# Encoder trunk with four token mixers on one core: where the transposes and value products stand in the opening of the MLA attention

## What is computed

```
hn = rms_norm(h, attn_norm_g[l])
proj = hn @ w_in[l]                      # 4 mixers read column groups of proj
y_a = mla_mixer(...)                     # 8 heads, latent attention
y_b = ssd_mixer(...)                     # Mamba-2, both directions
y_c = diff_mixer(...)                    # differential attention, 4 heads
y_d = mlstm_mixer(...)                   # chunkwise mLSTM, both directions, 4 heads
h = h + concatenate([y_a, y_b, y_c, y_d]) @ w_out[l]
hn = rms_norm(h, ffn_norm_g[l]);  gate, up = split(hn @ w_ffn_in[l])
h = h + (silu(gate) * up) @ w_ffn_out[l]
```

```
q = apply_partial_rope(rms_norm(q, q_head_g), cos, sin)
k = apply_partial_rope(rms_norm(k, k_head_g), cos, sin)
h = rms_norm(h, out_g).reshape(b, t, MLSTM_HEADS * MLSTM_V)
return jax.nn.sigmoid(o_raw) * h
```

## Time and profile before

| | before |
|---|---|
| median of 3 runs | 2541.05 us (2537.44 to 2541.64) |
| profiled execution, span from first to last instruction | 2538.3 us |
| PE busy | 2259.8 us (89%) |
| DVE busy | 1363.9 us (54%) |
| ACT busy | 888.2 us (35%) |
| POOL busy | 965.0 us (38%) |
| opening of layer 0, from the first query product to the first row maximum | 489.48 to 527.19 us |
| opening of layer 1, the same | 1765.86 to 1803.68 us |

### The profile page before, as it was taken

One profiled execution on the slowest core, in us unless ns is written; L12 is line 12 of the kernel. 1 busy time (PEld: TensorE's weight loads), 2 busy tenths in 40 slices (PEclk: granted clock), 3 DMA queues, 4 the chain that ended last, 5 costly groups with the idle time before them and its releaser, 6 DMA issues.

```text
span 2538.3 us, 34867 instructions
## 1 busy us (share of the span) xinstructions
PE 2259.8 (89%) x13988; PEld 1913.0 (75%) x13988; DVE 1363.9 (54%) x2245; ACT 888.2 (35%) x1476; POOL 965.0 (38%) x526
## 2 busy tenths in 40 slices
PE   7999888787877999999989999887878778999999
PEld 7867678655656999999989676686556557788887
DVE  8577765455556644442065687655555566544410
ACT  3333222256656222222223232222566563222221
POOL 4322323166421344444433223331664213444444
PEclk9999999989999999999999999999899999999999
DMA  4211111100000233333322111111000002323233
GB/s 149 69 34 42 42 34 34 51 9 1 25 18 18 68 92 92 91 88 97 100 75 76 34 34 42 34 42 50 9 1 17 26 17 67 92 92 100 91 101 115
DMA packets 40048, 143.94 MB, mean 57 GB/s; under 512 B 4432, under 2 KB 4560, under 8 KB 39760
## 3 DMA queue, kind: packets, MB, share of 16 engines
q1 hardware_dynamic: 39888, 141.72, 17.8%
HBM read 139.60 MB, written 2.10 MB: 56 GB/s over the span
## 4 chain that ended last, share of the span: by engine, by line
PE 67%; DVE 17%; ACT 8%; issue 6%; POOL 1%; DMA 1%; SPq 0%; ACTq 0%; DVEq 0%; POOLq 0%
PE pb L623 40%; PE pb L654 6%; PE pb L653 6%; PE pb L655 6%; PE pb L757 3%; DVE mbuf L1430 3%; ACT ebuf L1068 3%; DVE kh L1369 2%; PE pb L818 2%; PE pb L904 2%; DVE rowmax L1492 1%; ACT ebuf L1079 1%; ACT rstd L1036 1%; DVE ebuf L1414 1%; ACT rstd L1037 1%
## 5 line engine op out<-in xcount | busy, mean ns | idle before, releaser
L508 POOL TENSOR_TENSOR parts<-raw,parts 128x1024 fp32r<-128x1024 f32 x248 | 606.5, 2446 | 954.4 <-ACT parts L1119 954.1
L623 PE MATMUL pb<-mix,parts 128*128 128x264 f32 x4608 | 684.3, 295 | 30.3 <-POOL parts L508 21.7
L623 PEld LDWEIGHTS pb<-mix,parts 128*128 128x128 f32 x4608 | 614.7, 195 | 69.0 <-issue 46.6
L1119 ACT ACTIVATE parts<-raw 128x1024 fp32r<-128x1024 f32 x248 | 262.3, 1058 | 770.3 <-PE pb L623 468.7
L623 PE MATMUL pb<-proj_r,parts 128*128 128x264 f32 x3104 | 427.5, 285 | 0.5 <-POOL parts L508 0.5
L623 PEld LDWEIGHTS pb<-proj_r,parts 128*128 128x128 f32 x3104 | 399.6, 189 | 0.8 <-issue 0.7
L1045 ACT ACTIVATE ebuf<-ebuf 128x528 f32<-128x528 f32 (+4 forms) x240 | 111.0, 464 | 326.1 <-DVE ebuf L1414 199.5
L653 PE MATMUL pb<-proj_r,parts 128*128 128x512 f32 x528 | 207.6, 393 | 0.8 <-DVE mbuf L1351 0.8
L655 PE MATMUL pb<-proj_r,parts 128*128 128x512 f32 x528 | 207.8, 394 | 0.0
L654 PE MATMUL pb<-proj_r,parts 128*128 128x512 f32 x496 | 197.5, 398 | 0.0
L1357 DVE TENSOR_TENSOR h<-h,pb 128x528 f32<-128x528 f32 (+1 forms) x48 | 33.3, 694 | 271.2 <-PE pb L623 139.1
(11 more groups left out here) (217 smaller groups left out, 3301.9 us busy)
## 6 DMA issues: line engine op xcount, KB each, us to landing
raw<-w_stream SPq DMA_DIRECT2D x250, 512.0 KB, 3.6
w_head<-w_heads SPq DMA_DIRECT2D x8, 512.0 KB, 5.1
h<-x_t SPq DMA_DIRECT2D x8, 264.0 KB, 6.8
out_t<-h SPq DMA_DIRECT2D x8, 256.0 KB, 4.4
con<-consts SPq DMA_DIRECT2D x1, 1652.5 KB, 10.3
par<-params SPq DMA_DIRECT2D x1, 340.0 KB, 4.4
con<-consts SPq DMA_DIRECT2D x1, 128.0 KB, 6.8
```

What stands on the lines that cost most here:

```text
L508: nc.gpsimd.tensor_tensor(parts[:, n % PARTS, 1, :], w, parts[:, n % PARTS, 0, :].bitcast(FP32), ALU.subtract).then_inc(split.sem, 1)
L623: last = nc.tensor.matmul(pb[rows_, 2 * p + a, 0:HALF], lhs_t, rhs[:, a * HALF:(a + 1) * HALF], start=start, stop=stop)
L1119: nc.scalar.activation(parts[:, n % PARTS, 0, :], raw[:, r % RAW, :], ACT.Copy).then_inc(lead_ready.sem, 1)
```

## The change

The table is written in another order. No instruction is added or removed, and the semaphores and buffers are the same. All transposes and all value products now lie between the stages of head 0's preparation, and head 1's five stages come last, with nothing between them.

```diff
-        OPENING = (("p", 0, 0), ("p", 1, 0), ("t", 0, 0), ("t", 1, 0), ("p", 2, 0), ("t", 2, 0), ("p", 3, 0), ("t", 3, 0), ("t", 4, 0),
-                   ("p", 4, 0), ("v", 0, 0), ("v", 1, 0), ("p", 0, 1), ("p", 1, 1), ("v", 2, 0), ("v", 3, 0), ("p", 2, 1), ("v", 4, 0),
+        OPENING = (("p", 0, 0), ("t", 0, 0), ("t", 1, 0), ("t", 2, 0), ("p", 1, 0), ("t", 3, 0), ("t", 4, 0), ("v", 0, 0), ("p", 2, 0),
+                   ("v", 1, 0), ("v", 2, 0), ("p", 3, 0), ("v", 3, 0), ("v", 4, 0), ("p", 4, 0), ("p", 0, 1), ("p", 1, 1), ("p", 2, 1),
                    ("p", 3, 1), ("p", 4, 1))
```

## The result

| | before | the change |
|---|---|---|
| median | 2537.82 us (2533.49 to 2541.64, 6 runs) | 2544.99 us (2541.48 to 2546.70, 6 runs) |
| ratio to before, 95% interval | | 1.0031 (1.0017 to 1.0045) |
| span of the profiled execution | 2538.3 us | 2543.6 us |
| opening, layer 0 and 1 | 37.7 and 37.8 us | 38.1 and 42.1 us |
| half sum of head 0, from the same start | 64.9 and 65.0 us | 64.4 and 68.3 us |

A forecast was written before the change was run, and what follows sets the result against it. The prediction took a latency chain through DMA, PE, DVE and ACT in each layer's opening as the bound. At 2.7 us a layer, 5.4 in all, it forecast a median of 2546.5 us, range 2539.5 to 2552.

The forecast's parts named there:

- The forecast case: Opening: clock falls before head 1's key product, costing 2.7 us a layer, 5.4 in all; chance 0.50.
- The front is 1.9 us ahead in PE work: Opening up to head 1's first product: starts at 512.0, not 508.74, but with 5.1 us of value products already done.
- the walk: Link-by-link timing of the opening's front from 489.35, through transposes and value products, to head 1's first product at 512.0.
- The tail, link by link, 17.85 us at the low clock: Head 1's first product to row maximum: 17.85 us without value products, against 18.45 before with 5.1 us of them.
- that bound: Head 1's copy of 48 rows: taken as 1.0 us; 0.43 or 1.55 moves the cost 0.55 either way a layer.
- 2.7 us a layer at the row maximum: End of the opening: row maximum at 529.85 with the key product at the low clock, 2.7 us later than before.
- the shift is carried whole from there: Behind the opening: nothing between two waits takes up a shift, so all 5.4 us reach the kernel's end.
- The tail at the high clock, +0.8: Rival, head 1's tail: clock stays high up to the key product, +0.8 us a layer, 2541.5 to 2543.9; chance 0.27.
- The late rise: Rival, opening's front: clock rises only behind the first value product, 3.3 us a layer more, 2553 us; chance 0.13.
- Faster, if the clock holds throughout: Rival, tail and first attention steps: shorter gaps keep the clock high, -3.3 us a layer, 2534.4 us; chance 0.10.
- That the bare tail is the cause: Head 1's tail: waits that value products 2 to 4 filled before now stand empty; part of the 2.7 us a layer.

The follow-up runs named there:

- filled change: The change plus a useless product on PE ahead of head 1's stages 0, 2, 3 and 4; ratio 1.0018 (1.0007 to 1.0028) to the kernel before.
- the kernel with four products of no use at the start: The spread order plus four useless PE products in the wait for the heads' weights; ratio 0.9951 (0.9934 to 0.9968) to the kernel before.
- The first half of the change: Against the kernel before: transposes placed as in the change, value products left as before; ratio 1.0027 (1.0015 to 1.0039), 6.9 us slower.
- spread order: Table reordered against the kernel before, one or two transposes or value products in nearly every PE wait; ratio 0.9954 (0.9942 to 0.9965), median 2525.59 us.
- the kernel with the tail put back: The change with value products 2, 3 and 4 moved into head 1's three waits; ratio 0.9997 (0.9986 to 1.0009) to the kernel before.

## Why the prediction was right, step by step

The forecast case came true as put: slower, by waits left bare in head 1 and a clock that falls before the key product. The change's median of 2544.99 us lies in the range, and 5.4 us forecast stand against 7.9 (4.3 to 11.4). That 2546.5 came within 1.5 us of the median is in part luck: it was added to 2541.05, and six runs put the kernel before at 2537.82.

- *The front is 1.9 us ahead in PE work.* Head 1's first product started 23.4 us behind the first query product, where I had 512.0 - 489.48 = 22.5. `o_tok`'s scaling, the third transpose, the copy and the first value product came within 0.4 us of the walk; the rest crept in with a few tenths a link. The front was 0.9 us too early in my sum, so it is 1.0 ahead.
- *The tail, link by link, 17.85 us at the low clock.* Measured 18.4 (1791.07 to 1809.46). The copy of the 48 rows took 1.41 us, where I had taken 1.0; in layer 0 it took 0.46, so values near both ends of that bound occurred.
- *2.7 us a layer at the row maximum.* It was 4.2 where the clock fell, by these two terms. This is the step that was mis-sized. It was partly repaired by one that I had left out: in the change the low clock ends sooner behind the row maximum, 43 us behind the start and not 46, and the way to the half sum is 0.9 us shorter. My sentence that the shift is carried whole from there was wrong by those 0.9 us. Net 3.3, near 2.7 only because an error of +1.5 us and one of -0.9 partly cancel.
- *The tail at the high clock, +0.8.* Layer 0 of the first profile is this case: +0.4 at the row maximum, -0.5 at the half sum. I gave it 0.27, and it was one of four openings.
- *The late rise.* It did not come: the clock rose 5.2 to 5.7 us behind the start in all openings of the change, as before (5.2 to 5.6), with three tiles of transposes in between (489.78 to 492.94 us in layer 0, the rise at 493.1). By the rule on transposes in the Trainium skill ("TensorE: Matmul & The Clock Gate", Part 4) it would have come later; this case's traces do not agree.
- *Faster, if the clock holds throughout.* The -3.3 us a layer were far too many. Layer 1 of the filled change comes nearest to this case, with no low clock from the rise on, and its half sum is 64.5 us, 0.5 under before. It takes 26.3 us from row maximum to half sum, against 27.2: the low stretch before costs 0.9 us there, not 3. PE waits for ACT and DVE in these steps (1.47 us at 529.92 before), which may be why; no run tests it. The price hangs on where the low stretch lies: when it reaches 10.3 us behind the row maximum and not 8.5, as in the kernel with four products of no use at the start, it is 2.3 us (28.6 against 26.3).
- *That the bare tail is the cause* was too narrow, and the profile of the change alone would not have told. The first half of the change, with the old tail, is nearly as slow (6.9 us against 7.9, with intervals that overlap). An opening's PE work is the same in every order, so a step that moves covers one wait and can bare another: 6.9 us of waits before, 8.1 in the change, 2.0 in the spread order.

## What to carry to other kernels

In a chain that goes round several engines, list the waits of the engine with the filler work, and put one filler into each; here two fillers in one wait and none in the next lost much of one of them. Count what a row of bare waits does to the clock of the stretch behind it, and check a gain at a landmark well past the place of the change: here 2.3 of 2.7 us gained in a stretch were lost in the next. A few useless products in a wait are a cheap probe for the clock's share.

## What the hardware showed that I had not expected

Waits of 1.6 and 2.1 us, with 1 to 3 us of PE work between, brought the clock from its upper to its lower level (2.4 to 1.2 GHz, granted clock 1.00 to 0.50): at 19.2 to 19.4 us, within the second of two, in the kernel with the tail put back, and at 29.4 to 29.6 us, within the third of three, in three of four openings of the change. The Trainium skill ("TensorE: Matmul & The Clock Gate", "A second HAM failure mode: psum-queue depth-cycling") tells of a kernel in which short idles between groups of products, often repeated, made the clock go to and fro; the traces here agree, with idles of this size. The moment isn't fixed by the program: the same list of the change had the fall at 29.6 us in one layer and at 35.9 in the other. And products whose result nobody reads, put in waits, went with lower ratios: 1.0031 to 1.0018 in the change, 0.9954 to 0.9936 in the spread order. In both pairs the intervals overlap, so the gain is shown by the openings (42.0 to 38.2 us, 31.8 to 29.1) and not by time.
